# A transformer block with product-key experts: where the query products stand beside the expert gather, and when five gather buffers join

## The reference

```
mod = silu(c) @ w_ada + b_ada                      # 6 rows of 1024
h   = rms_norm(x) * (1 + scale1) + shift1
z   = h @ w_in                                     # q,k,v of two attention groups, two merge gates
x   = x + gate1 * (merge of both attentions @ w_out)
h2  = rms_norm(x) * (1 + scale2) + shift2
q   = (h2 @ w_q).reshape(T, 8 heads, 2, 128)       # "query products"
sc  = einsum('thpc,hpnc->thpn', q, sub_keys)       # 2 lists of 128 scores per head
s1, i1 = top_k(sc[:, :, 0], 16); s2, i2 = top_k(sc[:, :, 1], 16)
top_s, eid = best 16 of the 256 sums s1 + s2       # expert number 128 * i1 + i2
g   = softmax(top_s)
w   = g * gelu(h2 . u_tab[eid])                    # 128 experts per token
x   = x + gate2 * sum(w * v_tab[eid])
```

## Time and profile before

| | |
|---|---|
| median of three executions | 900.38 us |
| the profiled execution's own time | 899.82 us |
| its span, first to last instruction | 898.0 us |
| PE busy | 775.0 us (86%) |
| DVE busy | 613.8 us (68%) |
| ACT busy | 346.4 us (39%) |
| POOL busy | 288.4 us (32%) |
| data moved | 336.7 MB, 375 GB/s over the span |
| gather transfers | 268.45 MB |

### The profile page before, as it was taken

How to read it: one execution, slowest core, us unless ns; L and a number is a source line. 1 busy time by engine, 2 the same in 40 slices (tenths; PEclk the granted TensorE clock), 3 DMA queues, 4 the chain that set the end, 5 groups by cost and what they waited for, 6 DMA issues and landing times.

```text
span 898.0 us, 8443 instructions
## 1 busy us (share of the span) xinstructions
PE 775.0 (86%) x2526; PEld 417.6 (47%) x2526; DVE 613.8 (68%) x1422; ACT 346.4 (39%) x1027; POOL 288.4 (32%) x279
## 2 busy tenths in 40 slices
PE   4999999999999999999996868787777777777777
PEld 2477877667556656565652323333323232223232
DVE  6788798864587967749669788658644444444445
ACT  3458687862244342423234232322322222222222
POOL 4000000000254454443637334463443434333320
PEclk9999999999999999999999988898899999999999
DMA  9977544689499999999999999999999999999995
GB/s 375 424 280 282 178 196 188 252 337 383 161 381 423 408 423 421 415 420 422 421 420 422 422 421 420 422 422 420 422 422 421 421 422 421 421 421 423 421 421 203
DMA packets 44244, 336.70 MB, mean 375 GB/s; under 512 B 4900, under 2 KB 5284, under 8 KB 7464
## 3 DMA queue, kind: packets, MB, share of 16 engines
q0 software_dynamic: 37152, 268.45, 72.1%
q1 hardware_dynamic: 6888, 67.59, 19.1%
q10 hardware_dynamic: 160, 0.13, 0.0%
HBM read 335.11 MB, written 1.05 MB: 374 GB/s over the span
## 4 chain that ended last, share of the span: by engine, by line
PE 46%; DMA 36%; DVE 9%; ACT 3%; issue 2%; POOL 2%; another core or an unknown queue 1%; SPq 0%; DVEq 0%; ACTq 0%
DMA ring<-in_peer_uv,eid 32%; PE ps_y L1631 19%; PE bank L1604 5%; DMA rows<-in_peer_uv,eid 4%; PE bank L1570 3%; DVE ring L1025 3%; PE bank L1445 2%; PE bank L1446 2%; PE bank L1447 2%; PE bank L1585 2%; PE ps_y L1445 1%; PE ps_y L1409 1%; PE ps_y L1447 1%; PE ps_y L1446 1%
## 5 line engine op out<-in xcount | busy, mean ns | idle before, releaser
L1631 PE MATMUL ps_y<-ring,diag 128*128 128x512 f32 x568 | 275.5, 625 | 55.5 <-ACT diag L1316 54.4
L603 POOL DMA_INDIRECT ring<-in_peer_uv,eid x142 | 154.3, 1087 | 418.4 <-DVE eid L931 224.0
L1025 DVE CUSTOM_DVE_ANT_0 ring<-ring,gates 128x1024 f32<-128x1024 f32 x143 | 173.2, 1224 | 101.4 <-DMA ring<-in_peer_uv,eid 100.8
L1631 PEld LDWEIGHTS ps_y<-ring,diag 128*128 128x128 f32 x568 | 109.0, 198 | 203.3 <-issue 121.2
L1304 ACT ACTIVATE mask<-mask 128x2 f32<-128x2 f32 (+1 forms) x132 | 26.7, 202 | 358.6 <-DVE mask L1025 340.7
L1316 ACT ACTIVATE diag<-ident,mask 128x128 f32<-128x128 f32 x256 | 87.3, 387 | 0.3
L1631 PE MATMUL ps_y<-rows,diag 128*128 128x512 f32 x136 | 61.9, 598 | 7.6 <-ACT diag L1316 7.6
L1309 ACT ACTIVATE mask<-g_sb,mask 128x1 f32<-128x1 f32 x256 | 61.9, 287 | 4.3
L1025 DVE CUSTOM_DVE_ANT_0 rows<-rows,gates 128x1024 f32<-128x1024 f32 x34 | 41.3, 1224 | 31.1 <-DMA rows<-in_peer_uv,eid 31.0
L660 DVE TENSOR_TENSOR w_lo<-ring,w_hi 128x512 fp32r<-128x512 f32 x76 | 50.7, 685 | 10.3 <-PE bank L1447 8.8
L1121 ACT ACTIVATE w_hi<-ring 128x512 fp32r<-128x512 f32 x76 | 45.6, 627 | 22.6 <-PE bank L1447 22.2
(11 more groups left out here) (233 smaller groups left out, 1214.1 us busy)
## 6 DMA issues: line engine op xcount, KB each, us to landing
ring<-in_ada_t SPq DMA_DIRECT2D x11, 2048.0 KB, 9.4
ring<-in_in_t SPq DMA_DIRECT2D x10, 2048.0 KB, 9.9
ring<-in_up_t SPq DMA_DIRECT2D x2, 2048.0 KB, 7.8
ring<-in_out_t SPq DMA_DIRECT2D x2, 2048.0 KB, 10.8
ring<-in_peer_uv,eid POOLq DMA_INDIRECT x142
x_sb<-in_x SPq DMA_DIRECT2D x2, 1024.0 KB, 10.1
ring<-in_ada_t SPq DMA_DIRECT2D x2, 1024.0 KB, 21.0
kz<-in_peer_t SPq DMA_DIRECT2D x1, 2048.0 KB, 19.7
```

What stands on the lines that cost most here:

```text
L603: pool.indirect_dma_start(uv_row(n), None, peer_uv, bass.IndirectOffsetOnAxis(ap=eid[:, n:n + 1], axis=0)).then_inc(s_uv[name], 16)
L1025: dve.tensor_tensor_reduce(u_row(n), u_row(n), h2[:, n // P, :], 1.0, 0.0, ALU.mult, ALU.add, adot[:, at:at + 1]).then_inc(s_dot, 1)
L1631: ins = pe.matmul(ps_y[:, cut], diag[:, n % ND, :], v_row(n)[:, cut], start=first, stop=last)
```

## The change

Two tables of numbers are changed, no instruction is added or removed.

```diff
 SLOT = {
     "h2T1": 2,
-    "queries": ((None, 1, 3, 5, 13, 16, 25, 28), (7, 10, 19, 22, 31, 34, 37, 40)),
-    "keys": ((None, 2, 6, 18, 30), (42, 50, 58, 70)),
-    "pairs": ((None, 2, 8, 20, 32), (44, 52, 60, 72)),
-    "experts": ((None, 3, 10, 22, 34), (46, 54, 62, 74)),
+    "queries": ((None, 1, 3, 5, 13, 17, 28, 32), (8, 11, 21, 24, 37, 41, 45, 49)),
+    "keys": ((None, 2, 6, 18, 33), (42, 50, 58, 70)),
+    "pairs": ((None, 2, 8, 20, 35), (44, 52, 60, 72)),
+    "experts": ((None, 3, 10, 22, 37), (46, 54, 62, 74)),
 }
-           ("R1b", 0), ("W", 11), ("X", 12), ("V", 52), ("S", 53), ("E", 76), ("Ka", 88), ("Kb", 89)]
+           ("R1b", 0), ("W", 11), ("X", 12), ("V", 56), ("S", 57), ("E", 90), ("Ka", 106), ("Kb", 107)]
```

## The result

The changed kernel takes 901.93 us in the median of 18 executions (900.20 to 904.01), the kernel before, run beside it, 900.26 us in 18 executions (899.06 to 900.81). The ratio is 1.0022 with an interval of 1.0016 to 1.0028. Like all ratios here it isn't the quotient of the medians: it lies near that of the means, so an upper tail weighs more in it. The profiled execution of after took 901.11 us (span 899.3), against 899.82 before.

The account below looks back on a forecast made before the run. The prediction took the gather to be bound by its transfers to the end. Only V's late issue cost time: 899.8 + 3.0 = 902.8 us, 903.4 on the median's scale, with a range of 900.2 to 906.7.

Parts of the forecast that it names:

- The bound: Whole gather: transfers at 420 to 423 GB/s bound it; moving PE work matters only by opening or closing holes.
- Part 1: Products at slots 8, 11: PE idles 2.7 us at 295.8, is 2 us late; hole at 300 grows up to about 1 us.
- Part 2: Tile 0's m = 5 at slot 17: DVE starts choose_keys at 350.4, waiting 6.8 us; row 47's dot ends at 376.9.
- Part 3: V issued at 385.5, its first row now 56; that row's dot comes at 393.6; cost taken as 3.0 us.
- nothing gives the 3.0 us back: After row 56: the stream is full again and is the bound, so the 3.0 us stay to the end.
- V's hole: Stream near 387 to 392 us, from V's late issue: well under 400 GB/s, costing 3.0 us.
- The 8.1 us from issue to dot: Time a row needs when the queue has nearly run dry, used to put row 56's dot at 393.6.
- Part 4: Later products, E and Ka: issued early enough, Ka at 506.9 with 0 to 0.5 us more, taken as nothing.
- hidden hole: At V: a row issued 4 to 5 us ahead of its turn still lands in time; 900.5 to 901.9 us, chance 0.25.
- Fed better: At V: products moved back free places sooner, holes close or shrink; 898.8 us at best, chance 0.06.
- The clock: Behind PE's idle gaps at 295.8 and 356.5 the clock falls, adding 1.7 to 3.3 us; 905.1 to 906.7, chance 0.12.

Follow-up runs that it names:

- f2: The kernel before, with V and S joining at rows 56 and 57 instead of 52 and 53: 900.18 us, ratio 1.0000.
- f3: The kernel before, with the issue of row 232 delayed until row 226 has been added: 901.04 us in eight executions, ratio 1.0012.
- f4: The kernel before, with the issue of row 70 delayed until row 64 has been added: 903.29 us, ratio 1.0034.
- e3: The changed kernel, with tile 0's query product m = 5 back at slot 16 instead of 17: 901.12 us, ratio to before 1.0019.
- e1: The changed kernel, with V and S joining at rows 60 and 61 instead of 56 and 57: 901.06 us, ratio to before 1.0020.
- f1: The changed kernel, with tile 1's query product m = 0 back at slot 7 instead of 8: 900.15 us, ratio to before 1.0001.
- f6: The kernel before, with only tile 1's query product m = 0 moved from slot 7 to 8: 901.42 us, ratio 1.0018.
- e2: The changed kernel, with tile 1's query product m = 3 at slot 23 instead of 24: 901.17 us, ratio to before 1.0011.
- g2: The kernel before, with tile 1's m = 0 at slot 8 and 24 throwaway matmuls ahead of rows 14 and 15: 901.05 us, ratio 1.0005.
- g1: The changed kernel, with 24 throwaway matmuls ahead of rows 14 and 15: 902.56 us, ratio to before 1.0030.
- e4: The kernel before, with only tile 1's products m = 0 and m = 1 moved from slots 7, 10 to 8, 11: 903.95 us, ratio 1.0045.

## Why the prediction came out as it did

**The bound** (the gather's stream; only its holes count) is confirmed in part. Holes are where a change can act, but a hole's size in GB/s isn't its price: f2, f3 and f4 give nothing that can be seen, 1.0 and 3.2 us for 0.5, 4.4 and 4.6 us of missing transfers.

**Part 1** was right: gap 2.63 us (forecast 2.7), row 22 at 320.8 (320.6). The hole behind 300 us grew by about the 1 us that was allowed for it, all of it from 310 to 320 us.

**Part 2** was right: DVE reaches `choose_keys` at 350.55 (350.4) after waiting 5.90 us (6.8), and row 47's dot ends at 377.0 (376.9). e3 undoes it.

**Part 3** was right up to the hole. V at 385.64 (385.5); row 56's dot comes at 391.27, earlier than 393.6, but row 57's at 395.61, so that row 59 is 2.7 us late (3.0). The step that failed is the last: "nothing gives the 3.0 us back". That term is mis-sized. At the end of the profiled execution 1.3 us are left of it, and by the medians no more than half of that can be laid to it: taking V's hole away gives 0.7 us (after is 1.7 above before, e1 0.9; their ratios, 1.0022 and 1.0020, differ by 0.2 us and aren't told apart), and f1 keeps 1.5 us of hole at a price of 0.1, give or take 0.9. What takes the 3.0 us in is the lag between bytes and complete rows, which I had read as none because the GB/s were full. The 8.1 us from issue to dot were read from the third row behind V's; V's own row took 7.4 us (372.28 to 379.64).

**Part 4** was right. E is issued at 466.62, Ka at 508.02 (506.9), and no slice there is weak.

**The rivals.** The *hidden hole* (0.25) is wrong at its place, since rows 57 to 59 are late. The page "DMA: Bandwidth & Descriptors" of the Trainium skill (Anatomy of one DMA) gave an estimate of 4.4 us for a row, so a landing at 390.0 after the issue at 385.64. The row's dot came at 391.27, 5.6 us after the issue, and row 57's 4.3 us later instead of 2.5: the rule is 1.2 us short for the one transfer and misses the one behind it. A single transfer's duration didn't tell whether a queue that has run dry keeps up. Its result, a cost near nothing for V's hole, is nonetheless close to what was measured. *Fed better* (0.06) is wrong. *The clock* (0.12) was priced as a second case beside the hole, and the place of m = 0, which opens the gap for it, is in truth the larger part of the change: putting it back (f1, which also brings V 1.1 us earlier) takes the whole 1.7 us away, and f6, which has it without the rest, has a ratio of 1.0018. That it acts by the clock, and only in some executions, is what e2, f6 and g2 point to and what g1 leaves open for the changed kernel. Where the clock falls it costs more than the 1.7 to 3.3 us of the forecast: the profiled executions of e2 and f6 are 4.7 and 5.1 us above the shortest ones of the same kernels. I had taken a case that happens in part of the executions as a case that holds in all or in none. e2 and f6 show a fall directly behind the gap of 2.63 us, after and e1 none behind the same gap, and the page "TensorE: Matmul & The Clock Gate" of the Trainium skill (HAM oscillation) agrees in kind: there idle gaps of PE, longer ones than this, bring the clock down and the work behind them starts slow.

So the time, 1.5 us below the forecast, has the forecast sign, but less than half of it comes from the forecast cause. That the sign and the range hold is in good part luck: an overpriced hole stood in for a cost that the forecast's sum had at nothing. Forecast: 3.0 for the hole and 0 for the clock. Measured: 0.1 (f1) to 0.7 us (after against e1) for the hole, the rest of 1.7 for m = 0 at slot 8. Open are the share of each among after's 18 executions (only one has a profile), what makes the lag grow in steps, why g1 stays high, and why e4 is above f6.

## What to carry to other kernels

Before moving work of PE, look for the idle gap that it was hiding: the product at slot 7 cost nothing where it stood, and one slot later it left a gap behind which the clock was halved in two of the profiles. Such a cost is seen in the spread of many executions; the profile of a short one doesn't have it. Read the price of a hole in a transfer stream from the consumers' times at the end, not from GB/s; a stream at its full rate may still have a reserve between bytes and complete transfers, and the times of a transfer's semaphore increments show it. And test a suspected hole by making one of known size at that place and at another.

## What the runs showed of the hardware that was not expected

A gap of 2.63 us in PE's work was followed by a granted clock of 0.51 and 0.52 in two profiles (3.5 and 6.9 us long), and by 1.00 in those of after, e1 and e3, with the same order of work before it. Gather rows of 1.05 MB landed at 2.516 us each over 197 rows where the moved bytes gave 2.485, and the time from a row's first semaphore increment to its last grew from 2.4 us at row 56 to 7.2 at row 199 and 7.4 at row 233; a hole of 4.4 us brought it down from 6.9 to 1.3 us. And a queue that had run dry gave its second row 4.34 us after the first (391.27 to 395.61), then 2.46 us for the next (398.07).
